# A depthwise convolution moved from VectorE to TensorE in a two-layer hybrid decoder

## The reference

```python
def causal_dwconv(prefix, u, w, bias):
    L = u.shape[1]
    full = jnp.concatenate([prefix.astype(u.dtype), u], axis=1)
    y = bias
    for j in range(SSM_CONV):
        y = y + full[:, j:j + L] * w[j]
    return y, full[:, -(SSM_CONV - 1):]
...
    xbc_c, conv_state = causal_dwconv(conv_prefix, xbc, conv_w, conv_b)
    xbc_c = jax.nn.silu(xbc_c)
```

## Time and profile before

| | us |
|---|---|
| median of 3 executions | 2628.42 (2622.33 to 2630.66) |
| the profiled execution, its time | 2628.95 |
| its span, first to last instruction | 2627.2 |
| TensorE busy | 2441.3 |
| VectorE busy | 759.3 |
| ScalarE busy | 619.6 |
| GpSimd busy | 148.3 |

### The profile page before, as it was taken

How to read it: one execution, slowest core, us unless ns; L and a number is a source line. 1 busy time by engine, 2 the same in 40 slices (tenths; PEclk the granted TensorE clock), 3 DMA queues, 4 the chain that set the end, 5 groups by cost and what they waited for, 6 DMA issues and landing times. The chain is left out here.

```text
span 2627.2 us, 44029 instructions
## 1 busy us (share of the span) xinstructions
PE 2441.3 (93%) x19464; PEld 1563.0 (59%) x19464; DVE 759.3 (29%) x1250; ACT 619.6 (24%) x951; POOL 148.3 (6%) x157
## 2 busy tenths in 40 slices
PE   7997989788999999979897885999999999999999
PEld 5776667566777777766675664353535445453535
DVE  2355232431111013642324313314040422213122
ACT  2413364320345024134633201000000000000000
POOL 2011111001000000111110010000000000000000
PEclk9998888798999999987987986999999999999999
DMA  4432323334454444323233331999999999999994
GB/s 133 129 112 81 105 78 116 117 124 136 112 140 118 122 151 128 97 85 112 82 120 111 125 105 66 417 415 379 360 365 357 374 348 354 375 354 367 362 357 158
DMA packets 290398, 535.19 MB, mean 204 GB/s; under 512 B 10937, under 2 KB 222011, under 8 KB 273825
## 3 DMA queue, kind: packets, MB, share of 16 engines
q1 hardware_dynamic: 290208, 532.38, 57.4%
HBM read 518.50 MB, written 13.85 MB: 203 GB/s over the span
## 5 line engine op out<-in xcount | busy, mean ns | idle before, releaser
L862 PE MATMUL bank<-mem 128*32 128x256 f32 (+10 forms) x14512 | 1401.2, 442 | 53.7 <-DVE mem L1922 24.4
L862 PEld LDWEIGHTS bank<-mem 128*32 128x32 f32 (+3 forms) x14512 | 770.2, 125 | 648.3 <-issue 428.3
L862 PE MATMUL bank<-hflat,mem 128*128 128x288 f32 (+3 forms) x3088 | 759.2, 415 | 22.3 <-DVE hflat L1932 13.2
L862 PEld LDWEIGHTS bank<-hflat,mem 128*128 128x128 f32 (+2 forms) x3088 | 574.6, 192 | 195.3 <-issue 24.8
L1559 ACT ACTIVATE mem<-bank 128x288 f32<-128x288 f32 (+10 forms) x448 | 200.4, 465 | 1256.2 <-PE bank L862 654.3
L1559 ACT ACT_TABLE_LOAD x149 | 191.2, 1283 | 62.7 <-PE bank L862 59.4
L1922 DVE TENSOR_TENSOR xT<-xT,bank 128x288 f32<-128x288 f32 x88 | 35.7, 451 | 562.3 <-PE bank L862 562.3
L1559 ACT ACTIVATE mem<-mem 128x1152 f32<-128x1152 f32 (+9 forms) x217 | 158.4, 730 | 83.0 <-DVE mem L1982 36.3
L868 PE MATMUL bank<-ident,mem 128*128 128x128 f32 (+4 forms) x618 | 104.6, 314 | 51.6 <-DVE mem L1922 15.0
L1922 DVE TENSOR_TENSOR mem<-mem,bank 128x288 f32<-128x288 f32 (+3 forms) x180 | 90.5, 510 | 191.9 <-PE bank L862 105.6
L868 PEld LDWEIGHTS bank<-ident,mem 128*128 128x128 f32 (+4 forms) x618 | 79.7, 167 | 85.6 <-issue 45.4
(11 more groups left out here) (196 smaller groups left out, 808.3 us busy)
## 6 DMA issues: line engine op xcount, KB each, us to landing
mem<-in_w_moe_up_dram SPq DMA_DIRECT2D x64, 2048.0 KB, 10.2
mem<-in_w_moe_down_dram SPq DMA_DIRECT2D x56, 2048.0 KB, 10.5
mem<-in_w_moe_up_dram SPq DMA_DIRECT2D x32, 2304.0 KB, 10.0
mem<-in_w_in_dram SPq DMA_DIRECT2D x70, 1024.0 KB, 5.1
mem<-in_w_moe_up_dram SPq DMA_DIRECT2D x16, 1536.0 KB, 8.4
mem<-in_w_ffn_up_dram SPq DMA_DIRECT2D x44, 512.0 KB, 5.0
mem<-in_w_ffn_down_dram SPq DMA_DIRECT2D x16, 704.0 KB, 4.9
mem<-in_cache_kv_w_dram SPq DMA_DIRECT2D x20, 512.0 KB, 4.6
```

Source lines behind the costliest of these rows:

```text
L862: return mm(out, lhsT, rhs, start=start, stop=stop, skip_group_check=True)
```

## The change

VectorE builds, at the head of `hgrn_inputs`, 32 diagonal matrices of 128 x 128 for the layer: the identity times tap j of block m, one per partition (`conv_taps`). TensorE then convolves a block by four products that accumulate in one bank, each with a tap matrix as the stationary operand and `xpad` shifted by j as the moving one. ScalarE drains the bank with the bias. Two blocks are done in each of steps 0 to 3, behind `level`. VectorE's `convolve` is gone, and the signal `conv_done` with it.

```diff
@@ plan_mixer
+                if s < 4:
+                    acc_job(("conv", L, 2 * s))
+                    acc_job(("conv", L, 2 * s + 1))
@@ TensorE
+            def convolve(L, m):
+                acc = open_bank(("conv", L, m))
+                pe.wait_ge(*drained(("proj", L, 20 + m)))
+                if m == 0:
+                    pe.wait_ge(*drained(("cstate", L)))
+                    pe.wait_ge(*at("taps_ready", L))
+                for j in range(CONV):
+                    ins = put(acc[:, 0:CW], taps[CONV * m + j], xpad[:, m, j:j + CW], j == 0, j == CONV - 1)
+                close_bank(ins, ("conv", L, m))
...
+                    if s < 4:
+                        convolve(L, 2 * s)
+                        convolve(L, 2 * s + 1)
@@ ScalarE, in step s behind level_decay(L, s + 1)
+                    if s < 4:
+                        for m in (2 * s, 2 * s + 1):
+                            key = ("conv", L, m)
+                            act.wait_ge(*filled(key))
+                            empty(fn(cv[:, m, 0:CW], psum(key)[:, 0:CW], ACT.Identity,
+                                     bias=vecs[:, L, V_CB + m:V_CB + m + 1]), key)
                     if s == 4:
-                        act.wait_ge(*at("conv_done", L))
                         say(fn(cve[:, :, 0:CW], cv[:, :, 0:CW], ACT.Exp, scale=-1.0), "conv_exp", L)
@@ VectorE
             def hgrn_inputs(L):
+                conv_taps(L)
...
-                    if i < 4:
-                        for m in (2 * i, 2 * i + 1):
-                            convolve(L, m)
...
+            def conv_taps(L):
+                for m in range(KT):
+                    for j in range(CONV):
+                        ins = ve.tensor_scalar(taps[CONV * m + j], ident[:, :],
+                                               vecs[:, L, V_CW + 8 * j + m:V_CW + 8 * j + m + 1], None, ALU.mult)
+                        step(ins) if (m, j) != (KT - 1, CONV - 1) else say(ins, "taps_ready", L)
```

More of the change, by code:

```diff
@@ L66 @@
     vexp_ready=4, s0_scaled=4, hg_osq=1, hg_rstd=1, hg_done=1,
-    conv_done=1, conv_exp=1, conv_plus=1, conv_sig=1, z_plus=1, z_sig=1, gate_plus=12, gate_sig=12, xs_ready=1, conv_tail=1, z_exp=1, z_gated=1,
+    taps_ready=1, conv_exp=1, conv_plus=1, conv_sig=1, z_plus=1, z_sig=1, gate_plus=12, gate_sig=12, xs_ready=1, conv_tail=1, z_exp=1, z_gated=1,
     dt_neg=1, dt_log=1, dt_cum=1, dt_exp=1, dt_ready=1,
@@ L143, in hybrid_decoder @@
         zexp = view(arena, 14720 + 8 * PADT, 4, T)
+        taps = [view(arena, 11480 + P * i, P) if i < 25 else view(over, 34 * T + P * (i - 25), P) for i in range(8 * CONV)]
+        assert 11480 >= A1 + 3200 and 11480 + 25 * P <= 14720
         cve = view(over, 42 * T, 8, PADT)
@@ L2059, in gate_plus @@
                 plus(gates[:, 2 * k:2 * k + 2, :], "gate_plus", L, k + 1)
[L2061 to L2072, removed]
+            def conv_taps(L):
[4 more added lines that the diff above has]
+                        step(ins) if (m, j) != (KT - 1, CONV - 1) else say(ins, "taps_ready", L)
             def new_conv_rows(L):
+                for t in (25, 26, 27):
+                    dve.wait_ge(*drained(("proj", L, t)))
                 step(ve.tensor_copy(ctail[:, :, 0:TAIL], xpad[:, :, PADW - TAIL:PADW]))
```

## The result

| | before | changed |
|---|---|---|
| median, us | 2628.9 (4 runs) | 2646.69 (4 runs, 2644.46 to 2652.27) |
| span of the profiled execution, us | 2627.2 | 2642.7 |

The ratio is 1.0081 with a 95% interval of 1.0056 to 1.0106. The forecast was 2647 us, range 2639 to 2655.

What follows compares the result with a forecast made beforehand. TensorE, busy for 93% of the span, was taken as the bound, so added work is paid in full. Products of 16.9 us less 7.8 us of gains, 1.3 + 4.5 + 2.0, per layer gave +18.2 us: 2647 us, range 2639 to 2655.

Steps and rivals of the forecast that it cites:

- The sum: Per layer: 16.9 us of added products less 1.3, 4.5 and 2.0 us, +9.1 us; for two layers +18.2 us.
- An exposed load: Rival on TensorE's products: weight loads not hidden, 0.909 us per product, 24.4 us more, 2671.6 us; chance 0.03 if fully exposed.
- The waits: TensorE's waits for VectorE before levels 3 and 4 both go, gaining 1.3 + 4.5 = 5.8 us per layer.
- the 20.9 us behind it: From the exponentials' end to level 6: addition, masks, decay, sigmoid, product, `lvl_q`; said to stay 20.9 us.
- steps 4 to 6: Start of level 4 to start of level 6: `conv_exp` starts earlier, 24.8 us instead of 26.8, gain 2.0 us.
- The wait before level 6: TensorE's wait behind the sigmoid's chain stays, some 5.3 us, with the slow clock after it.
- The taps: 32 tensor_scalar on VectorE, 0.33 us each, 10.6 us per layer, hidden; 1.9 us of cover left in layer 0.
- No change: Rival: the wait before level 6 goes too, with the slow clock behind it; 2630.5 us, chance 0.06.
- The faster rival: From level 3 to the recurrence's tail, added products only fill waits; 2614 us if all 24.5 us vanished, chance 0.03.
- the slow clock behind level 4: Term of the faster rival: time that the slow clock adds behind level 4, put at 2 us.

Runs made afterwards that it cites:

- the early convolution: Kernel before, convolution still on VectorE but all eight blocks in round 0 instead of two in each of rounds 0 to 3: 2609.82 us, ratio 0.9935.
- the one with a single tap: Changed kernel with only tap 0's product of the four in each block's convolution, all tap matrices and drains kept: 2621.74 us, ratio 0.9976.
- the kernel in which that wait was taken out on purpose: Changed kernel with VectorE's product with the convolution's sigmoid moved from round 5 to round 6: 2632.19 us, ratio 1.0023.

## Why the prediction was right

**The bound.** TensorE's added work was paid in full: 16.8 us per layer by the comparison with the early convolution, 0.525 us per product by the one with a single tap. The sum had 16.9 and 0.529. That was argued from the projection's pace and scaled by columns; the shifted start of the moving operand costs nothing to be seen.

**The weight load.** An exposed load would have made 0.909 us per product. By the rule of "TensorE: Matmul & The Clock Gate" (the Trainium skill, section "Part 3: Packing small matmuls — row/col tiling") that was to be feared; the measurement of 0.525 us decides against it here, for f32 products with 312 columns. The same section of the Trainium skill also lets a load go ahead when it targets the background weight buffer, which the prediction didn't weigh. Which way these loads take, no run here shows.

**The waits.** Those before levels 3 and 4 went, as said, with the slow clock behind the second. From the start of level 4 to that of level 6 the changed kernel takes 243.15 - 218.16 = 25.0 us; the sum had 24.8, and 26.8 before. `conv_exp` ends at 222.25 us, 4.1 us after level 4 could start where 3.9 were worked out, and the 20.9 us behind it came back to the tenth. ScalarE's timeline, against the earlier trace rows:

```profile
...
218.42 0.41 ACT L1577 ACTIVATE mem<-bank 128x288 f32<-128x288 f32 x1 [3.47 <-PE bank L867]
218.87 3.38 ACT L1577 ACTIVATE mem<-mem 128x1024 f32<-128x1024 f32 x2
...
229.37 1.06 ACT L1577 ACTIVATE mem<-mem 128x1024 f32<-128x1024 f32 x1 [0.99 <-DVE mem L2006]
...
```

ScalarE no longer waits 6.54 us for VectorE's distances ahead of the pair of exponentials. Per layer, from level 0 to level 6, that makes 83.46 us against 74.70, +8.8 us where the sum had +9.1, and 17.5 us for both layers. By the runs its terms are +16.8 for the products, -6.2 for the two waits and -1.8 for steps 4 to 6. The sum had the waits at their idle time, 5.8 us; but without them the kernel with the early convolution takes 41.67 us from level 0 to level 4 where the kernel before takes 47.89, so they cost 0.4 us more than they show as idle. (The 16.4 us of work less 5.8 us of waits in the stretches above are the same 10.6 us, split otherwise.)

The profiled execution is only 15.5 us longer than that of before. It was 2.2 us shorter between level 6 and the tail (17.25 us against 18.52 in layer 0, 17.04 against 17.97 in layer 1), where the clock came back sooner after the wait. That is no gain of the change: the projection behind level 6 took 7.92 us here and 8.98 us in the kernel with one product, whose program is the same from there on. The medians differ by 17.8 us. That the median came within 0.3 us of the forecast is in part luck: the terms were off by some tenths in both directions, and the four executions of the changed kernel cover 7.8 us.

**The wait before level 6** was said to be some 5.3 us and is 5.73. VectorE's timeline of the changed kernel, against the earlier trace rows:

```profile
...
237.74 6.62 DVE L1945 TENSOR_TENSOR mem<-mem 128x2048 f32<-128x2048 f32 x11 [6.93 <-ACT mem L1577]
...
```

The row is the product with the sigmoid, with `lvl_q` of level 6 as its last part but one. The experiments show what the wait is: VectorE's wait for the sigmoid ahead of `lvl_q`. It didn't change with 12.6 us less work of TensorE before level 4, and it went when only the product was moved.

**The taps.** The estimate was 0.33 us each from the comparison with a column. VectorE's and ScalarE's timelines in layer 0:

```profile
...
52.91 10.28 DVE L2085 TENSOR_SCALAR mem<-ident,vecs 128x128 f32<-128x128 f32 x32
63.22 0.76 DVE L1949 TENSOR_SCALAR mem<-mem 128x1152 f32<-128x1152 f32 x1
...
```

```profile
...
64.06 1.28 ACT L1577 ACT_TABLE_LOAD   x1 [3.66 <-DVE mem L1949]
...
69.03 0.85 ACT L1577 ACTIVATE mem<-bank 128x288 f32<-128x288 f32 x2
...
71.63 0.41 ACT L1577 ACTIVATE mem<-bank 128x288 f32<-128x288 f32 x1 [0.55 <-PE bank L867]
...
```

They take 10.28 us, 0.32 each. ScalarE starts its sigmoid at 64.06 us, 3.66 us late, and catches up by tile 8 (0.55 us of idle time left before 71.63 us). TensorE has no wait there. With the taps twice as long it has one of 8.26 us.

**The chances.** No change had 0.06 and faster 0.03. "No change" by the end of the wait before level 6 was priced at 2630.5 us; the kernel in which that wait was taken out on purpose measured 2632.19. The faster rival needed products that fill the waits before level 6 and the tail; both waits stood, for the reason given, that the products are ahead of those chains. A version with the products placed inside the wait before the tail wasn't tried. In that rival's sum the slow clock behind level 4 was put too low: level 4 takes 3.78 us and the projection behind it 8.90 instead of 7.93 us, which makes 2.8 us and not 2. Its time and chance hardly depend on it.

## What to carry to other kernels

An engine at 30% load that makes the busy one wait is first asked where its work stands, not which engine should do it: here VectorE had 29.8 us of idle time ahead of the masks of level 0, and moving two lines of its program gave back 17.6 us, while moving the work to the bound engine cost 17.8. Work added to the bound engine is priced by count times the pace of its nearest products, and only the waits that it removes, with the slow clock behind them, are set against it. Of a wait that is left, ask which instruction queued ahead of the needed one is itself waiting; here moving that one instruction group gave 14.5 us.

## What the runs showed of the hardware

A VectorE tensor_tensor is held by GpSimd's product, as scalar_tensor_tensor was before. VectorE's and GpSimd's timelines of the changed kernel, before level 2, and VectorE's of the kernel before at the same place:

```profile
...
178.40 1.05 DVE L2023 COPY_PREDICATED mem<-lmask,bank 128x512 f32<-128x512 uint32 x2 [0.16 <-PE bank L867]
179.49 4.58 DVE L1945 TENSOR_TENSOR mem<-mem 128x1152 f32<-128x1152 f32 x2
...
```

```profile
...
178.84 2.62 POOL L801 TENSOR_TENSOR mem<-mem 128x1152 f32<-128x1152 f32 x1 [14.04 <-PE bank L867]
...
```

```profile
...
180.16 2.75 DVE L1922 TENSOR_TENSOR mem<-mem 128x1152 f32<-128x1152 f32 x2
...
```

The two tensor_tensor (`lvl_q` and the difference) take 4.58 us, against 2.75 us where GpSimd is idle, 1.8 us more; GpSimd's product runs on for 2.0 us after their start. It is `lvl_q`, the first of them, whose end is put off: GpSimd's product ends at 181.46 us and leaves the second at most 0.6 us in which it could be held. Masks that read PSUM aren't held (0.73 us either way). Three rounds of two layers make 11 us of VectorE's busy time, which is why it fell by 17.8 and not by 28 us. It cost nothing here, since TensorE comes later.

ScalarE's drain with the bias from a column takes longer than columns explain, so that ScalarE gained 8.4 us and not 7. Groups by line of the changed kernel:

```profile
...
L1577 ACT ACTIVATE mem<-bank,eps 128x288 f32<-128x288 f32 x38 | 19.1, 501 | 9.0 <-PE bank L867 8.4
...
L1577 ACT ACTIVATE mem<-bank,vecs 128x312 f32<-128x312 f32 x16 | 8.4, 522 | 37.9 <-PE bank L867 37.9
...
```

The drain takes 522 ns. A plain copy of 288 columns takes 0.41 us and one of 384 columns 0.49 us, which makes 0.43 us for 312, an estimate. An activation of 288 columns that takes its bias from the column `eps` needs 501 ns, 90 ns more than the copy. "ScalarE: Activation LUTs" of the Trainium skill, section "What ACT_TABLE_LOAD costs", says that a per-partition pointer operand adds about 93 ns to an activation. An estimate by that is 0.52 us for the drain; the trace agrees.
